# A fused two-block transformer on one core: gate tiles moved between the steps of linear attention, inner features kept in PSUM

## What is computed

```python
# first block
h = x + hybrid_mixer(rmsnorm(x))          # spatial gating | conformer conv | mLSTM cells
h = h + cross_attention(rmsnorm(h), rmsnorm(mem))
h = h + conv_glu(rmsnorm(h))              # (gelu(conv3(up_a)) * up_b) @ w_down, inner width 2816
x = rmsnorm(h)
# second block, layer 0: NSA + pooling, then MLP;  layer 1: GLA, then MLP
x = layer_norm(ALPHA * x + mix)
x = layer_norm(ALPHA * x + square(relu(x @ w1)) @ w2)        # inner width 4096

# spatial gate
s = einsum('hts,bcshd->bcthd', tril(w_s), vn) + b_s          # then u * s
# GLA, 4 heads, chunks of 64 tokens
o = att @ v + q_t @ state_before;  state = decay * state + upd
o = o * rsqrt(mean(o * o)) * norm_g;  out = (o * silu(r)) @ w_out
```

## Time and profile before

| | us |
|---|---|
| median of three runs | 2102.74 |
| the profiled execution | 2101.9 |
| its span, first to last instruction | 2100.1 |
| TensorE busy | 1958.1 (93%) |
| VectorE, ScalarE, GpSimd busy | 1046.7, 393.2, 1119.0 |
| mean granted TensorE clock | 0.966 |

### The profile page before, as it was taken

The page is one execution under the profiler, slowest core; times in us unless marked ns, Lnnn a source line. Parts: engine busy times, 40 slices in busy tenths (PEclk is TensorE's granted clock), DMA queues, the critical chain, the costliest instruction groups (busy, mean ns, idle before and its releaser), DMA issues.

```text
span 2100.1 us, 24689 instructions
## 1 busy us (share of the span) xinstructions
PE 1958.1 (93%) x8970; PEld 1563.9 (74%) x8970; DVE 1046.7 (50%) x1376; ACT 393.2 (19%) x733; POOL 1119.0 (53%) x622
## 2 busy tenths in 40 slices
PE   5989998899999999988989999998998889999997
PEld 4857776578888877877778888887776468888885
DVE  3953332348458184147667255267131368164466
ACT  3313222121011013024330000013221221000012
POOL 4733655148676585630046676665663056676662
PEclk9989999899999999999999999999997899999998
DMA  5311322014332234320022333322332022233331
GB/s 195 112 59 51 100 81 81 22 61 119 91 98 91 80 120 153 120 61 1 11 71 81 99 101 100 100 81 81 98 91 63 0 81 81 80 103 98 108 91 40
DMA packets 46875, 175.99 MB, mean 84 GB/s; under 512 B 5200, under 2 KB 5328, under 8 KB 46032
## 3 DMA queue, kind: packets, MB, share of 16 engines
q1 hardware_dynamic: 46368, 168.05, 26.2%
q10 hardware_dynamic: 432, 6.88, 0.8%
HBM read 172.81 MB, written 2.10 MB: 83 GB/s over the span
## 4 chain that ended last, share of the span: by engine, by line
PE 46%; DVE 2%; ACT 1%; POOL 1%; issue 1%; POOLq 0%; DVEq 0%; ACTq 0%
PE acc L459 8%; PE acc L457 8%; PE acc L458 8%; PE acc L480 5%; PE acc L481 5%; PE acc L484 5%; PE acc L505 1%; PE acc L507 1%; PE acc L506 1%; PE misc L943 1%; POOL w_lo L2102 1%; PE acc L959 0%; DVE h L1552 0%; PE acc L963 0%; PE misc L528 0%
## 5 line engine op out<-in xcount | busy, mean ns | idle before, releaser
L2100 POOL TENSOR_SCALAR w_hi<-raw 128x1024 fp32r<-128x1024 f32 x309 | 358.1, 1159 | 923.1 <-PE acc L484 477.6
L2102 POOL TENSOR_TENSOR w_lo<-raw,w_hi 128x1024 fp32r<-128x1024 f32 x309 | 766.0, 2479 | 25.8
L457 PE MATMUL acc<-x_hi,w_hi 128*128 128x512 f32 x864 | 340.0, 394 | 0.0
L459 PE MATMUL acc<-x_hi,w_lo 128*128 128x512 f32 x864 | 336.8, 390 | 0.0
L458 PE MATMUL acc<-x_lo,w_hi 128*128 128x512 f32 x864 | 336.6, 390 | 0.0
L1576 DVE TENSOR_TENSOR h<-acc,h 128x512 f32<-128x512 f32 x120 | 82.9, 691 | 346.6 <-PE acc L459 274.2
L457 PE MATMUL acc<-y_hi,w_hi 128*128 128x512 f32 x638 | 250.4, 392 | 3.3 <-DVE y_lo L1978 1.8
L459 PE MATMUL acc<-y_hi,w_lo 128*128 128x512 f32 x638 | 248.6, 390 | 0.0
L458 PE MATMUL acc<-y_lo,w_hi 128*128 128x512 f32 x638 | 248.6, 390 | 0.0
L459 PEld LDWEIGHTS acc<-x_hi,w_lo 128*128 128x128 f32 x864 | 162.3, 188 | 33.8
L457 PEld LDWEIGHTS acc<-x_hi,w_hi 128*128 128x128 f32 x864 | 162.5, 188 | 32.1
(11 more groups left out here) (343 smaller groups left out, 2690.8 us busy)
## 6 DMA issues: line engine op xcount, KB each, us to landing
raw<-weights_dram SPq DMA_DIRECT2D x309, 512.0 KB, 3.6
w_cmp<-w_cmp_dram ACTq DMA_DIRECT2D x1, 4096.0 KB, 15.6
h<-x_dram SPq DMA_DIRECT2D x2, 1024.0 KB, 9.8
out_dram<-h SPq DMA_DIRECT2D x8, 256.0 KB, 2.0
small<-small_dram ACTq DMA_DIRECT2D x1, 1536.0 KB, 9.0
...
const<-const_dram SPq DMA_DIRECT2D x1, 576.0 KB, 11.9
```

The lines of the kernel that those rows point to most:

```text
L457: mm(out, m["w_hi"][:, slot, k], hi[:, k], start=k == 0, stop=False)
L459: last = mm(out, m["w_lo"][:, slot, k], hi[:, k], start=False, stop=k == kc - 1)
L2100: nc.gpsimd.tensor_scalar(hi, m["raw"][:, slot], 1.0, 0.0, ALU.mult, ALU.add).then_inc(sem("weights_high"), 1)
L2102: nc.gpsimd.tensor_tensor(m["w_lo"][:, slot].rearrange("p k n -> p (k n)"), m["raw"][:, slot], bf(hi), ALU.subtract).then_inc(sem("weights ...
```

## The change

- Start: weight tile 0 is loaded before const, tile 1 before par, and small1 last, on SyncE's queue. TensorE multiplies constants twice before the first norm's sum and twice after it (`idle_products`).
- Spatial gate: the bias of both heads and all tokens is one product of two rows with a broadcast operand; the sixteen L598 go.
- Masks: w_s is masked by a comparison in VectorE; the cells' second spreading and the mask products go. VectorE adds the diagonal's mask and bias (`cell_diagonal`), ScalarE's exp follows.
- Up projections: squares, convolutions and products are written back into the bank, ScalarE copies the bank to y_hi, VectorE subtracts from the bank for y_lo. `tile_out` is counted only then.
- GLA: the gate r is made feature-major by `r_tile`, each tile between two steps; the state updates stand inside the first four. The gate is applied after the turn (`gla_gain`), and the split comes after that, from SBUF. ScalarE's silu stands between rsqrt steps, so the function table is switched back (`logs`) four times.

```diff
-    for half in range(2):
-        add_wide(c_in[:, 2 * D + half * 512:2 * D + (half + 1) * 512], 512)
+    for c in range(KC):
+        add(c_in, slice(2 * D + c * P, 2 * D + (c + 1) * P))
...
+        "ident": np.eye(P), "causal_T": np.where(r[:, None] <= r[None, :], 0.0, NEG),
...
+        "half_sel": r[None, :] // 64 == np.arange(2)[:, None]})
...
+    def idle_products(n):
+        for _ in range(n):
+            mm(acc[:, 0], ones, m["const"][:, 0:S], start=True, stop=True)
+    idle_products(2)
     sum_squares("mix")
+    idle_products(2)
     opening(0, 0, "mix")
...
+        mm(misc[:, 2 + c], half_sel[0:2], b_s[0:2, blk(c)].unsqueeze(1).to_broadcast([2, TB, P]), start=True, stop=False)
         for tb in range(TB):
             for hh in range(2):
                 head = 2 * c + hh
-                out = misc[blk(hh, 64), 2 + c, blk(tb)]
-                mm(out, m["v_tok"][:, tb, blk(head, 64)], ws[:, head], start=True, stop=False)
-                last = mm(out, ones[0:1, 0:64], b_s[0:1, blk(head)], start=False, stop=True)
+                last = mm(misc[blk(hh, 64), 2 + c, blk(tb)], m["v_tok"][:, tb, blk(head, 64)], ws[:, head],
+                          start=False, stop=tb == TB - 1)
...
-        pe.wait_ge(sem("w_off"), head + 1)
-        mm(acc[:, 3], row_sel[0:4, head], m["row_M"][0:4], start=True, stop=False)
-        for sb in range(TB):
-            last = mm(acc[:, 3, blk(sb)], m["causal_h"], m["ident_h"], start=False, stop=sb == TB - 1)
-        last.then_inc(sem("M_masked"), 1)
         pe.wait_ge(sem("qkv_out"), 3 * head + 2)
...
-        opening_of(t0 + 2 * n, START["glu0"] + 2 * n, y_hi, y_lo, "glu_hidden", "glu_hidden", g * 8, kc=n)
+        opening_of(t0 + 2 * n, START["glu0"] + 2 * n, y_hi, y_lo, "glu_high", "glu_hidden", g * 8, kc=n)
...
-        opening_of(t0 + 8, START[name] + 8, y_hi, y_lo, hidden, hidden, g * 8)
+        opening_of(t0 + 8, START[name] + 8, y_hi, y_lo, high, "tile_out", g * 8, ready_before=t0)
...
+    def r_tile(c, beside=None):
+        t = START["gla_in"] + 17 + c
+        slot = t % RING
+        out = acc[:, 1 - c % 2]
+        pe.wait_ge(sem("weights_split"), t + 1)
+        pe.wait_ge(sem("tile_out"), START["gla_in"] + (14, 17)[c] if c < 2 else t - 1)
+        for k in range(KC):
+            mm(out, m["w_hi"][:, slot, k], x_hi[:, k], start=k == 0, stop=False)
+            mm(out, m["w_hi"][:, slot, k], x_lo[:, k], start=False, stop=False)
+            last = mm(out, m["w_lo"][:, slot, k], x_hi[:, k], start=False, stop=k == KC - 1)
+            if k == KC - 1:
+                last.then_inc(sem("tile_done"), 1)
+            if beside:
+                beside(k)
...
     def gla_updates(head):
-        pe.wait_ge(sem("gla_kd"), head + 1)
-        for n in range(7):
+        def beside(k):
+            if k == 0:
+                return
+            n = k - 1
             i = 7 * head + n
+            if n == 0:
+                pe.wait_ge(sem("gla_kd"), head + 1)
             if i >= 2:
                 pe.wait_ge(sem("gla_state"), i - 1)
             mm(misc[:, 1 + i % 2, 0:256], m["kd_tok"][blk(n % 2, 64), head % 2, n // 2],
                m["v_g"][blk(n % 2, 64), n // 2, blk(head, 256)], start=True, stop=True).then_inc(sem("gla_update"), 1)
+        return beside
...
-    pe.wait_ge(sem("tile_out"), END["gla_in"])
+        c = 2 * head + e
+        if c in (0, 7):
+            pe.wait_ge(sem("gla_att"), 8)
+        else:
+            pe.wait_ge(sem("gla_gained"), c)
+        bank = misc[:, c // 7]
+        for tb in range(TB):
+            last = turn(bank[:, blk(tb)], m["y_tok"][:, tb, blk(e)], ident)
+        last.then_inc(sem("gla_y_turned"), 1)
+    def feature_beside(head, e, step):
+        def beside(k):
+            if k == step:
+                gla_feature(head, e)
+        return beside
     gla_scores(0)
-    gla_updates(0)
+    r_tile(0, gla_updates(0))
     gla_scores(1)
-    gla_updates(1)
+    r_tile(1, gla_updates(1))
     gla_out(0)
     gla_scores(2)
-    gla_updates(2)
-    gla_feature(0)
+    r_tile(2, gla_updates(2))
+    gla_scores(3)
     gla_out(1)
-    gla_scores(3)
-    gla_updates(3)
-    gla_feature(1)
+    gla_feature(0, 0)
+    last_updates = gla_updates(3)
+    def updates_and_feature(k):
+        if k == 2:
+            gla_feature(0, 1)
+        last_updates(k)
+    r_tile(3, updates_and_feature)
+    gla_feature(1, 0)
     gla_out(2)
-    gla_feature(2)
+    gla_feature(1, 1)
+    r_tile(4)
     gla_out(3)
-    pe.wait_ge(sem("gla_y"), 6)
-
-    def turn_last(k):
-        if k == 6:
-            gla_feature(3)
-
-    normed_stage("gla_out", "ln1b", "gla_high", "gla_y", turn_last)
-    mlp("mlp_b", "ln1b", "mlp_b_hidden", "ln2b")
+    r_tile(5)
+    gla_feature(2, 0)
+    r_tile(6, feature_beside(2, 1, 3))
+    gla_feature(3, 0)
+    r_tile(7, feature_beside(3, 1, 5))
+    pe.wait_ge(sem("tile_out"), END["gla_in"] - 1)
+    normed_stage("gla_out", "ln1b", "gla_high", "gla_y")
+    mlp("mlp_b", "ln1b", "mlp_b_high", "ln2b")
...
-    act.dma_start(m["small1"], pr.dram["small1"]).then_inc(sem("small1_in"), 16)
...
     def weights_diagonal(head):
-        act.wait_ge(sem("M_masked"), head + 1)
         for sb in range(TB):
-            f(m["w_c"][:, sb, blk(sb)], acc[:, 3, blk(sb)], ACT.Exp, bias=m["g_col"][:, sb, head:head + 1])\
-                .then_inc(sem("w_exp"), 1)
+            act.wait_ge(sem("w_masked"), 4 * head + sb + 1)
+            f(m["w_c"][:, sb, blk(sb)], m["w_c"][:, sb, blk(sb)], ACT.Exp).then_inc(sem("w_exp"), 1)
...
     def glu_group(g, t0, n, norm=None):
-        act.wait_ge(sem("tile_out"), t0)
         for j in range(n):
             t = t0 + 2 * j
-            slot = (START["glu0"] + 2 * j) % RING
+            gate, up = ((START["glu0"] + 2 * j + i) % RING for i in range(2))
+            act.wait_ge(sem("tile_done"), t + 1)
             act.wait_ge(sem("glu_conv"), g * 8 + (j + 1))
-            out(t, slot, m["g_in"][:, j % 2, CONV_F - 1:])
+            f(m["g_in"][:, j % 2, CONV_F - 1:], acc[:, gate], ACT.Copy).then_inc(sem("glu_in"), 1)
             act.wait_ge(sem("glu_conv"), g * 8 + (j + 3))
-            f(m["g_act"][:, j % 2], m["g_act"][:, j % 2], ACT.Gelu).then_inc(sem("glu_gelu"), 1)
-            if j >= 2:
-                act.wait_ge(sem("glu_hidden"), g * 8 + (j - 1))
-            out(t + 1, (slot + 1) % RING, z[:, (slot + 1) % RING])
+            act.wait_ge(sem("tile_out"), t)
+            f(m["g_act"][:, j % 2], acc[:, gate], ACT.Gelu).then_inc(sem("tile_out"), 1)
+            act.wait_ge(sem("glu_product"), g * 8 + (j + 1))
+            f(m["y_hi"][:, j], acc[:, up], ACT.Copy).then_inc(sem("glu_high"), 1)
...
+                act.wait_ge(sem("tile_done"), t + 1)
                 if j >= RING:
-                    act.wait_ge(hidden, g * 8 + (j - RING + 1))
-                out(t, slot, z[:, slot], ACT.Relu)
+                    act.wait_ge(sem(name + "_product"), g * 8 + (j - RING + 1))
+                f(z[:, slot], acc[:, slot], ACT.Relu).then_inc(sem(name + "_relu"), 1)
+                act.wait_ge(sem(name + "_product"), g * 8 + (j + 1))
+                f(m["y_hi"][:, j], acc[:, slot], ACT.Copy).then_inc(sem(name + "_high"), 1)
...
+    def r_out(c):
+        t = t0 + 17 + c
+        out(t, None, m["r_g"][c], ACT.Silu, src=acc[:, 1 - c % 2])
     gla_kd(0)
+    r_out(0)
     gla_kd(1)
+    r_out(1)
+    logs()
+    gla_kd(2)
     gla_rstd(0)
-    gla_kd(2)
-    gla_high(0)
+    r_out(2)
+    logs()
+    gla_kd(3)
     gla_rstd(1)
-    gla_kd(3)
-    gla_high(1)
+    r_out(3)
+    logs()
     gla_rstd(2)
-    gla_high(2)
+    r_out(4)
+    logs()
     gla_rstd(3)
-    gla_high(3)
+    for c in range(5, KC):
+        r_out(c)
+    for c in range(KC):
+        act.wait_ge(sem("gla_gained"), c + 1)
+        f(m["y_hi"][:, c], m["r_g"][c], ACT.Copy).then_inc(sem("gla_high"), 1)
...
+    def cell_diagonal(head):
+        dve.wait_ge(sem("w_off"), 3 * head + 3)
+        dve.wait_ge(sem("row_cols_out"), 1)
+        for sb in range(TB):
+            if head:
+                dve.wait_ge(sem("p_c"), 4 * head)
+            v.scalar_tensor_tensor(m["w_c"][:, sb, blk(sb)], acc[:, 3, blk(sb)], m["g_col"][:, sb, head:head + 1],
+                                   pr.view("causal_T"), ALU.add, ALU.add).then_inc(sem("w_masked"), 1)
...
+            gate, up = (acc[:, (START["glu0"] + 2 * j + i) % RING] for i in range(2))
+            src = m["g_in"][:, j % 2]
+            dve.wait_ge(sem("glu_in"), g * 8 + (j + 1))
+            step.link(v.tensor_scalar(gate, src[:, 0:S], scalar(conv_w[:, 0], j), scalar(conv_bias, j),
+                                      ALU.mult, ALU.add))
+            step.link(v.scalar_tensor_tensor(gate, src[:, 1:S + 1], scalar(conv_w[:, 1], j), gate, ALU.mult, ALU.add))
+            v.scalar_tensor_tensor(gate, src[:, 2:S + 2], scalar(conv_w[:, 2], j), gate, ALU.mult, ALU.add)\
+                .then_inc(sem("glu_conv"), 1)
             dve.wait_ge(sem("tile_out"), t + 1)
```

(63 more changed lines are left out.)

109 lines of the change are left out of this document (37 added, 72 removed).

## The result

The changed kernel takes 2044.87 us in the median of four runs (2043.18 to 2047.45), the kernel before, run beside it, 2102.72; the ratio is 0.9727, with a 95% interval of 0.971 to 0.9744. It is faster by 57.9 us. The profiled execution took 2043.18 us, its span 2041.4: 58.7 us less than the span of before. The forecast was 2049 us, and 53.1 us on the profiled execution.

What follows compares the result with a forecast made beforehand. TensorE, busy 93% of the span, was taken as the bound. Terms 7.4 + 10.5 + 5.4 + 8.3 + 3.5 + 18 = 53.1 us off 2101.9 gave 2048.8, forecast as 2049; range 2033 to 2065 (2040 to 2056 at 0.58).

Steps and rivals of the forecast that it cites:

- The start: Start to first opening's end: opening 5.2 us earlier, 2.2 from constant products; 7.4 us won, bounds 3 to 9.
- The 2.2 us for the clock: First opening: constant products keep TensorE at work before it, so its 72 matmuls run at full pace; 2.2 us won.
- The spatial gate: Spatial gate: one bias product and 16 L597 at 0.33 us replace the alternation; 10.5 us won, bounds 5.8 to 15.
- The cells: Cells: second spreading and mask products go, less 0.6 for the clock; 5.4 us won, bounds 3.5 to 6.3.
- Up projections, MLP: MLP stages: gaps before down projections go as GpSimd splits weights faster; 8.3 us won, bounds 4 to 8.3.
- the rule of the bank: Up projections: a tile's path holding its bank costs time only from 3.9 us on; 4.9 would eat all won.
- The gated unit: Gated unit's up projections: last gate tile's path of 4 us fits behind a 5.45 us tile; 3.5 won, bounds 0 to 3.6.
- Linear attention: Linear attention and gate tiles: new order takes 99.8 us instead of 118.7; 18 us won, bounds 9 to 30.
- The 1 us for low clock: Linear attention: 1 us taken off the 18.9 won, for a stretch of low clock at its start.
- The updates hide: Rival, linear attention and gate: updates cost 0.38 us each, gate partly at full clock; 13 us less, 2036; chance 0.20.
- The heads pace it: Rival, linear attention: TensorE waits for each head's chain in three heads; 13 us more, 2062; chance 0.18.
- The banks are held too long: Rival, up projections: GpSimd blocks VectorE's PSUM operations, tile path 5.6 us; 2175, slower than before; chance 0.03.

Runs made afterwards that it cites:

- start_alone: The kernel before with only the start's edit: new order of first transfers and two pairs of constant products; 2095.05 us, ratio 0.9974.
- held: The changed kernel with three more VectorE operations on the way of every MLP up tile, its bank held meanwhile; 2073.88 us.
- gelu_pre: The changed kernel with the gelu's table loaded ahead of the gated unit's loop; 2045.42 us.
- pairs: The changed kernel with its state updates two behind every second chunk instead of one behind each; 2034.31 us, ratio 0.9677.
- no_idle: The changed kernel without its four constant products at the start; 2044.70 us, ratio 0.9735.

## Why the prediction was right, step by step

**The start** (7.4). The opening begins 5.3 us earlier, as worked out (5.2). The 2.2 us for the clock are there in start_alone and in four kernels built on the changed one, but not in the changed kernel's profiled execution (0.5). The products don't so much keep the clock up as bring it up early: the trace's first record of a full clock stands at 30.71 us in the kernel before, inside its opening, and at 16.88 in start_alone, ahead of it. The step holds. What it left out is the wait behind the last constant product, 1.7 to 2.9 us: where it was longest, the clock fell.

**The spatial gate** (10.5; 11.9). The mechanism is right, one size was off. The bias product took 1.97 us (2.0 forecast), but a product of v_tok 0.24 at half clock, not 0.33. The lower bound, 0.28, came from L930 at full clock and was no lower bound. The wait for v_tok stayed at 5.86.

**The cells** (5.4; 7.8). The spreading and mask that went account for 2.4 + 3 x 1.3 = 6.3 us. The rest fits the clock, which recovers at 141.5 us, 1.5 behind the gate's end, where in the kernel before it did so at 163.8, 6.1 behind it. I took 0.6 off for the clock where something had to be added: the sign of that term was wrong.

**Up projections, MLP** (8.3; 10.5). All eight gaps went, and w_lo stands at 2.40 among up tiles (2.63 in the earlier trace rows). The groups of the changed kernel, 1080 to 1107 us (busy us, mean ns, idle before and who ended it):

```profile
L2164 POOL TENSOR_TENSOR w_lo<-raw,w_hi 128x1024 fp32r<-128x1024 f32 x7 | 16.8, 2398 | 0.6
...
L2039 DVE TENSOR_TENSOR acc<-acc,z 128x512 f32<-128x512 f32 x7 | 4.9, 696 | 17.5 <-ACT z L1389 17.5
L2041 DVE TENSOR_TENSOR y_lo<-acc,y_hi 128x512 fp32r<-128x512 f32 x7 | 4.8, 692 | 4.7 <-ACT y_hi L1391 4.7
```

0.69 us each, as taken from L1576. The failed size is what a gap costs: I counted its idle time (0.98). But in the kernel before the last matmul ahead of such a gap and the first behind it start 1.37 us apart, where the pace is 0.23, and the next came 0.33 later: 1.25 us a gap.

```profile
1135.76 0.39 PE L459 MATMUL acc<-x_hi,w_lo 128*128 128x512 f32 x1
1137.13 0.49 PE L480 MATMUL acc<-y_hi,w_hi 128*128 128x512 f32 x1 [0.98 <-POOL w_lo L2102]
1137.46 0.40 PE L481 MATMUL acc<-y_hi,w_lo 128*128 128x512 f32 x1
```

8 x 0.27 more than the idle time is 2.2 us, the difference. The way of a tile was put at 2.9 us and is 1.96, because the next relu runs beside it. That changed nothing, as the rule of the bank (held) has its point at 3.9.

**The gated unit** (3.5; 1.7). This step failed. "4 us, less than the 5.45 of the up tile behind it" left out ScalarE's table loads: the way of the first gate tile is 0.6 + 2.7 + 1.28 + 0.6 us behind a first load of 1.28. The trace of before has loads in the same two groups (at 467.75 and 599.61 us for the gelu), where no wait of TensorE names the gelu; the change put the second one on the way of a bank. gelu_pre shows it.

**Linear attention** (18; 18.1). Right in the sum, by terms that offset each other. Forecast and measured: wait for k_g 2.4 and 2.4; scores and turns 4.8 and 4.1; gla_out 19.4 and 18.9; turns of y 4.8 and 3.2 (0.4 us each); updates 20.4 and 23.4; waits inside 1.3 and 1.1, the first turn's for att_g alone; the end 3.1 and 2.7 (1.3 for y_hi, 1.4 for y_lo). The mis-sized term is the update, 0.84 and not 0.73: my 0.10 for a change of shape was read from shapes that differ in columns (128*64), and the change in rows (64*128) costs 0.39. The 1 us for low clock was not needed, as the stretch stands at 1.00, but it made up for something else: the measured terms come with the tiles' 43.6 to 99.4 us, and the stage took 118.7 - 18.1 = 100.6. The 1.2 between are small delays where a tile takes over from another shape (0.32 us from its first matmul to the next instead of 0.23, at 1535.41), for which there was no term.

**The rivals.** "The updates hide" falls with the 0.84, though pairs reaches its 2036 us in another way. "The heads pace it": no wait for y_tok, r_g or rstd_g. "The banks are held too long": VectorE's new operations take 0.69 us beside GpSimd, and held shows where it would have begun.

**What the prediction had no term for.** The three rows at the foot of the table: stages without an edit gave 2.9 us net, in terms of up to 3.7. By the clock, the cross attention stood at 0.84 from 356 to 398 us in the kernel before and at 0.96 from 331 to 369 in the changed one. No row of before could tell which way that would go, and no_idle lost it again. The stretch before, then changed:

```profile
356.00:398.00 42.00, 30.77 (x88) 17.54 (x88) 18.59 (x50) 9.65 (x25) 0.00 (x0) 0.84 0.00 0
```

```profile
331.00:369.00 38.00, 26.84 (x88) 15.44 (x88) 18.80 (x50) 9.02 (x24) 0.00 (x0) 0.96 0.00 1
```

**Luck in the total.** The edited stages missed their terms by -1.6, +1.4, +2.4, +2.2, -1.8 and +0.1 us. These offset to +2.7, and the stages without an edit added 2.9. That the total came within 5.6 us of the forecast's 53.1 is in part this offsetting; the largest single term, the linear attention, was right in its sum only.
